# A two-block layer kernel: how the gated attention outputs of blocks one to three are turned from tokens to channels

## The chip, the cores and the metric

The kernel is one program on one core of a Trainium2 chip. The metric is the device time of one launch in microseconds (us). The engines that matter here are TensorE (PE in the rows; its weight load is PEld), VectorE (DVE), ScalarE (ACT), GpSimd (POOL) and SyncE (SP). POOL and SP issue DMA transfers; an engine works its own instructions off in order, and waits between engines go over semaphores.

## The reference, cut to what matters

The reference is a gated delta-rule and convolution block followed by a second block with latent attention. Only the second block's attention branch is touched:

```
h = rmsnorm(x, g);  proj = h @ w_in                      # z_mla is one 2048 wide part of proj
attn = causal_attention(q, k, v)                         # (256 tokens, 16 heads x 128)
attn = attn.reshape(256, 2048) * silu(z_mla)             # the gated attention output
y_mla = attn @ w_o_mla                                   # contracts over the 2048 channels
y_conv = (b_gate * conv * silu(z_conv)) @ w_o_conv
merged = sigmoid(g_mla) * y_mla + sigmoid(g_conv) * y_conv
x = x + rmsnorm(merged @ w_out, g_post)
```

Everything is float32, 256 tokens, model width 2048.

## The kernel before

**Matrix products.** Each product with a 2048 x 2048 weight is cut into 4 column blocks of 512, and each block into 8 *halves*: a half is two row tiles (2 x 128 rows) by 512 columns. A half is 12 matmuls of 128x512: two row tiles, two token tiles of 128, and three products each (hi x hi, hi x lo, lo x hi), since every float32 operand is carried as a high and a low float32r part. The activations stand in `r1h`/`r1l` or `r2h`/`r2l` (128 channels on the partitions, 16 channel tiles, 256 tokens).

**Weights.** SP loads chunks of 1 MB (two halves) into four buffers `raw`; it loads a chunk when DVE is done with the one four before. For each half ACT copies `raw` to `w_hi` (`split` in the scalar block) and DVE writes `w_lo` = `raw` - `w_hi` (`split` in the vector block). In step `hl` of a phase both do the split of half `hl + 3` first (`ahead`, LEAD = 3) and then the other work of that step. ACT may start the split of half h only when PE has finished half h-4 (`w_used`); PE starts half h only when its `w_lo` is there (`lo_ready`).

**The phases around the change**, in PE's order: FC (four rounds; attention heads and the short convolution), FG (gates), FZ (32 halves, the projection z_mla, operand `r2`), YM (32 halves, `w_o_mla`, operand `r1` = the gated attention output), YC (32 halves, `w_o_conv`, operand `r2` = the convolution result, read back from DRAM), OUT (32 halves, operand `r1` = the merged result). "Half 16" below means FZ's half with hl = 16; YM's halves are counted on from FZ's as 32, 33 and so on.

**The work on one block j of z_mla**, before. `at_block(hl, lag)` is j where hl = 8j + 8 + lag. In step 8j+8 ACT makes the tanh of the block's sums from PSUM into `thz` (`half_tanh`, two instructions). In step 8j+9 DVE multiplies (`attn_gate`: two instructions for `gated`, two more with the attention output of the block, which POOL has loaded into `oin[:, j % 2]`), and raises `m_ready`. After half 8j+10 PE waits for `m_ready` and makes 8 transposes of 128x128 (`merged_tr`, through `channels_first`) into two PSUM banks. In step 8j+11 ACT copies them to `r1h` (`merged_hi`) and DVE subtracts into `r1l` (`merged_lo`). For block three (j = 3) these steps fall on halves 32 to 35, that is on the first four of YM. YM's half q (q < 8) waits until `m_lo` shows that channel tiles 2q and 2q+1 are ready.

**The other way of turning.** In YC (and in YA/MIX of the first block) blocks 0 to 2 go another way: POOL writes the 256 x 512 tile to DRAM (`turn_spill`), waits for that write, and reads it back with four transfers (`turn`, `read_quarters`), so that 32-token groups stand on the partitions; one DVE instruction then transposes all 32 x 32 squares (`turned`, 128x1024). The weight columns that make the tile are permuted on the host so that this gives whole channel tiles. ACT's `turned_hi` and DVE's `turned_lo` then make the two parts from SBUF. There ACT and DVE take the tile at lag 7, `turned_lo` at lag 9.

**POOL's order** in FZ: load the four attention blocks into `oin` (the third and the fourth each wait for a block's transposes), load the gain of the last norm, then `reload` the convolution operand into `r2` in four steps, each when PE has gone past half 25, 27, 29 or 31 of FZ.

Of the kernel before, what the change touches and what calls it, by code (L numbers as in the profile page):

```python
# [24 lines left out]
P = 128  # L25
TOK = 256
TT = TOK // P
D = 2048
# [30 lines left out]
TURNS_YC = TURNS_FC + 2 * NJ  # L59
MTR_YA, MTR_ATTN, MTR_Y = 0, 1, 1 + NJ  # L60
# [177 lines left out]
def build_layer(nc, t, out):  # L238
# [38 lines left out]
    with ctx:  # L277
# [145 lines left out]
        with ExitStack() as st:  # L423
            s1 = lambda n, shape, dt=F32: sb(n, shape, dt, st)
            thm, thc = s1("thm", [P, TT, D]), s1("thc", [P, TT, D])
            oin = s1("oin", [P, 2, TT, NB])
            thz = s1("thz", [P, TT, NB])
            assert nc.sbuf_base <= own_end
# [3 lines left out]
        mtmpT = us[:].rearrange("p t h d -> p (t h d)").rearrange("p (a n) -> p a n", a=CT)  # L432
        yT = oin[:, 1].rearrange("p t n -> p (t n)").rearrange("p (a n) -> p a n", a=CT)
# [125 lines left out]
        def _(pool):  # L559
# [267 lines left out]
            pool.wait_ge(sem("m_tr"), MTR_YA + 1)  # L827
# [73 lines left out]
        def _(act):  # L901
# [394 lines left out]
            for hl in range(ph.hn):  # L1296
                ahead(ph, hl)
                if hl == 2:
                    turned_hi(r2h, mtmpT, NJ - 2, OP_M, NJ - 1)
                    merged_hi(r2h, NJ - 1, OP_M, MTR_YA + 1)  # L1300
                if at_block(hl, 0) is not None:
                    mix_block(at_block(hl, 0))
# [199 lines left out]
            for hl in range(ph.hn):  # L1502
                ahead(ph, hl)
                if at_block(hl, 7) is not None and hl < ph.hn - 1:
                    turned_hi(r1h, yT, at_block(hl, 7), OP_Y, NJ - 1 + at_block(hl, 7) + 1)
# [8 lines left out]
            for hl in range(ph.hn):  # L1514
                ahead(ph, hl)
                if hl == 2:
                    turned_hi(r1h, yT, NJ - 2, OP_Y, 2 * (NJ - 1))
                    merged_hi(r1h, NJ - 1, OP_Y, MTR_Y + 1)
                if at_block(hl, 0) is not None:
                    out_block(at_block(hl, 0))  # L1520
# [11 lines left out]
        def _(dve):  # L1532
# [742 lines left out]
            for i in range(ph.iters):  # L2275
                for hl in range(ph.hn):
# [34 lines left out]
                    if hl == 24:  # L2311
                        dve.wait_ge(sem("pv_done"), i + 1)
                        dve.wait_ge(sem("ost_free"), i + 1)
                        sig(V.tensor_tensor(th(ost), banks(0), over(rec[:].rearrange("p t h -> p (t h)"), VD), ALU.mult), "ost_ready", i + 1)
# [70 lines left out]
            for hl in range(PH["YC"].hn):  # L2385
# [5 lines left out]
                if at_block(hl, 7) is not None and hl < PH["YC"].hn - 1:  # L2391
                    merged_turned(yT, oin[:, 0].rearrange("p t n -> p (t n)"), TURNS_YC, at_block(hl, 7), NJ - 1)
# [14 lines left out]
            for hl in range(ph.hn):  # L2407
# [5 lines left out]
                if hl == 1:  # L2413
                    merged_turned(yT, oin[:, 0].rearrange("p t n -> p (t n)"), TURNS_YC, NJ - 2, NJ - 1)
# [30 lines left out]
        def _(pe):  # L2445
# [505 lines left out]
            def heads_tr(hl):  # L2951
                j = at_block(hl, 2)
                if j is not None:
# [66 lines left out]
```

## Time and profile before

| | |
|---|---|
| three runs | 2430.29, 2431.39, 2432.84 us; median 2431.39 |
| the profiled execution's own time | 2431.26 us |
| its span | 2429.7 us |
| mean granted TensorE clock | 0.997 |
| PE busy | 2386.9 us (98%) |
| PEld, DVE, ACT, POOL busy | 1965.0, 1627.4, 1130.7, 225.9 us |
| DMA | 503.68 MB, mean 207 GB/s |

The span is what the trace covers, 1.6 us less than the execution's time. A PE that is busy 98% of the span is followed in almost every half by the next half without a gap, so what an edit is worth shows in two ways only: instructions that leave PE or come to it, and gaps that open or close on PE.

### The profile page before, as it was taken

How to read it: one execution, taken by the hardware profiler on the slowest of the kernel's cores; microseconds unless marked ns; L12 is line 12 of the kernel's file. 1: busy time of each engine (PE TensorE's matmuls, PEld its weight loads, DVE VectorE, ACT ScalarE, POOL GpSimd, SP SyncE). 2: the span in 40 equal slices, each digit the busy share in tenths (PEclk: the TensorE clock that was granted, in tenths of full speed). 3: DMA queues.
4: the chain of work that ended last, by engine and by line, in shares of the span. 5: the costliest groups of instructions: out<-in, count | busy, mean ns of one | idle time of the engine just before them, and what ended most of it. 6: DMA issues, size and time to landing. Idle time of an engine off the chain costs nothing.

```text
span 2429.7 us, 34099 instructions
## 1 busy us (share of the span) xinstructions
PE 2386.9 (98%) x13315; PEld 1965.0 (81%) x13315; DVE 1627.4 (67%) x2173; ACT 1130.7 (47%) x1457; POOL 225.9 (9%) x391
## 2 busy tenths in 40 slices
PE   7999999999999999999999999999999999999998
PEld 6878878787878787878888788888888888888886
DVE  5799999878676776655656665757666544554564
ACT  5444444465453545343455564444444444443443
POOL 3000001112110203011000000010101000000100
PEclk9999999999999999999999999999999999999999
DMA  7566667666454546569655566677667756685673
GB/s 231 194 210 199 199 198 235 220 197 216 156 166 152 186 141 214 185 217 317 224 191 190 168 203 216 223 238 234 217 226 236 245 194 191 208 277 191 223 245 121
DMA packets 237420, 503.68 MB, mean 207 GB/s; under 512 B 14777, under 2 KB 15650, under 8 KB 236130
## 3 DMA queue, kind: packets, MB, share of 16 engines
q1 hardware_dynamic: 214082, 418.57, 52.6%
q0 software_dynamic: 23200, 83.17, 10.5%
q8 instruction: 99, 1.62, 0.3%
q14 instruction: 39, 0.32, 0.0%
HBM read 462.88 MB, written 38.81 MB: 206 GB/s over the span
## 4 chain that ended last, share of the span: by engine, by line
PE 58%; DVE 1%; ACT 1%; DMA 1%; issue 0%; POOL 0%; DVEq 0%; POOLq 0%; ACTq 0%
PE acc L2461 52%; PE acc L2481 2%; PE aux L2644 1%; PE aux L2523 1%; PE acc L2496 0%; PE aux L2924 0%; ACT w_hi L911 0%; DMA qT<-turn_spill 0%; DVE w_lo L1546 0%; DMA turn_spill<-kbe 0%; DVE thm L2428 0%; PE aux L2929 0%; PE aux L2509 0%; DVE kbe L1580 0%; DVE kbe L2031 0%
## 5 line engine op out<-in xcount | busy, mean ns | idle before, releaser
L1546 DVE TENSOR_TENSOR w_lo<-raw,w_hi 128x1024 fp32r<-128x1024 f32 x790 | 963.9, 1224 | 726.5 <-ACT w_hi L911 714.4
L911 ACT CAST w_hi<-raw 128x1024 fp32r<-128x1024 f32 x790 | 826.0, 1050 | 1117.9 <-PE acc L2461 1082.1
L2461 PE MATMUL acc<-w_hi,r1h 128*128 128x512 f32 (+1 forms) x1840 | 728.8, 396 | 8.0 <-DVE w_lo L1546 5.4
L2461 PE MATMUL acc<-w_lo,r1h 128*128 128x512 f32 (+1 forms) x1840 | 714.7, 388 | 0.0
L2461 PE MATMUL acc<-w_hi,r1l 128*128 128x512 f32 (+1 forms) x1840 | 714.4, 388 | 0.0
L2461 PE MATMUL acc<-w_hi,r2h 128*128 128x512 f32 x1208 | 472.3, 391 | 0.3 <-DVE r2l L1641 0.3
L2461 PE MATMUL acc<-w_hi,r2l 128*128 128x512 f32 x1208 | 470.2, 389 | 0.0
L2461 PE MATMUL acc<-w_lo,r2h 128*128 128x512 f32 x1208 | 470.1, 389 | 0.0
L2461 PEld LDWEIGHTS acc<-w_hi,r1h 128*128 128x128 f32 x1840 | 346.0, 188 | 88.0 <-DVE w_lo L1546 8.6
L2461 PEld LDWEIGHTS acc<-w_hi,r1l 128*128 128x128 f32 x1840 | 346.0, 188 | 72.6
L2461 PEld LDWEIGHTS acc<-w_lo,r1h 128*128 128x128 f32 x1840 | 346.4, 188 | 66.6
L2461 PEld LDWEIGHTS acc<-w_hi,r2h 128*128 128x128 f32 x1208 | 226.8, 188 | 48.5 <-issue 1.3
L2461 PEld LDWEIGHTS acc<-w_hi,r2l 128*128 128x128 f32 x1208 | 226.7, 188 | 47.5
L2461 PEld LDWEIGHTS acc<-w_lo,r2h 128*128 128x128 f32 x1208 | 226.8, 188 | 46.3
L1710 DVE SCALAR_TENSOR_TENSOR ycur<-upad,pcw,ycur 128x256 f32<-128x256 f32 x464 | 193.9, 478 | 0.2
L1830 DVE SCALAR_TENSOR_TENSOR cy<-cpad,wq,cy 128x256 f32<-128x256 f32 x144 | 60.7, 480 | 1.0
L2481 PE MATMUL acc<-r1h,w_hi 128*128 128x256 f32 x128 | 36.3, 284 | 1.7 <-DVE r1l L1641 1.7
L2481 PE MATMUL acc<-r1h,w_lo 128*128 128x256 f32 x128 | 36.2, 283 | 0.0
L2481 PE MATMUL acc<-r1l,w_hi 128*128 128x256 f32 x128 | 36.2, 283 | 0.0
L573 POOL TENSOR_SCALAR stat<-stat 128x2 f32<-128x2 f32 (+1 forms) x9 | 5.2, 581 | 306.4 <-DVE stat L2165 94.5
L2481 PEld LDWEIGHTS acc<-r1h,w_hi 128*128 128x128 f32 x128 | 24.5, 192 | 2.1 <-DVE r1l L1641 1.9
L662 POOL DMA_DIRECT2D gate_spill<-gtA x4 | 2.2, 545 | 251.1 <-ACT gtA L1000 251.1
(490 smaller groups left out, 1602.2 us busy)
## 6 DMA issues: line engine op xcount, KB each, us to landing
raw<-in_w_in SPq DMA_DIRECT2D x264, 1024.0 KB, 5.1
raw<-in_w_out SPq DMA_DIRECT2D x32, 1024.0 KB, 5.2
raw<-in_w_br_b SPq DMA_DIRECT2D x16, 1024.0 KB, 5.1
raw<-in_w_br_a SPq DMA_DIRECT2D x16, 1024.0 KB, 7.2
raw<-in_w_ple_gate SPq DMA_DIRECT2D x16, 1024.0 KB, 5.0
raw<-in_w_o_mla SPq DMA_DIRECT2D x16, 1024.0 KB, 5.1
raw<-in_w_o_conv SPq DMA_DIRECT2D x16, 1024.0 KB, 5.0
raw<-in_w_q_b SPq DMA_DIRECT2D x8, 1024.0 KB, 5.0
```

The costliest lines, as they stand in the source:

```text
L573: c.link(g.tensor_scalar(dst, src, scale, EPS, ALU.mult, ALU.add))
L662: pool.dma_start(gate_dram[kind, bass.ds(i, 1)].rearrange("a p n -> p (a n)"), tile[:].rearrange("p t n -> p (t n)")).then_inc(sem("gate_o ...
L911: nc.scalar.copy(w_hi[:, h % HL, 0:n], raw[:, k % RAW, x * HALF:x * HALF + n]).then_inc(hi_ready, 1)
L1546: V.tensor_tensor(w_lo[:, h % HL, 0:n], raw[:, k % RAW, x * HALF:x * HALF + n], w_hi[:, h % HL, 0:n].bitcast(F32), ALU.subtract).then_inc( ...
L1710: c.inc(V.scalar_tensor_tensor(out if k == TAPS - 1 else cur, win, w[:, k:k + 1], cur, ALU.mult, ALU.add))
L1830: c.inc(V.scalar_tensor_tensor(cy[:, h], win, w, cy[:, h], ALU.mult, ALU.add))
L2461: ins = T.matmul(acc[:, s, x, 0:n], a[:, kt0 + k, xs_], w[:, h % HL, at], start=start and k == 0 and m == 0, stop=stop and k == kts - 1 an ...
L2481: ins = T.matmul(acc[:, s, a // 2, a % 2 * TOK:(a % 2 + 1) * TOK], w[:, h % HL, at], o[:, kt0 + k, :], start=start and k == 0 and m == 0 a ...
L2523: ins = T.transpose(X[:, bank + a // 2, (a % 2) * TOK + x * P:(a % 2) * TOK + (x + 1) * P], src(x, a), ident[:])
L2644: ins = T.matmul(X[r, bank, m * SEQ_CHUNK:(m + 1) * SEQ_CHUNK], lhsT(x, h, r), rhs(x, h, r), start=True, stop=True)
```

## The change

The attention outputs of blocks 0 to 2 now go through `turn` as well, and only block 3 keeps PE's transposes. In the order of the program:

- The host permutes the first three 512-column blocks of z_mla's weights, and in FC DVE writes the normalised attention output of rounds 0 to 2 in that permuted order, with two instructions of 128x512 (one for each token tile) in place of one of 128x1024.
- POOL loads attention blocks 0 and 1, then for j = 0, 1, 2: waits for `m_ready` of block j, writes the gated tile to DRAM, waits for the write, reads it back into a new tile `h_land`; and for j = 1, 2 waits for `m_lo` of block j-1 and loads attention block j+1. Only then, and after the transposes of block 3, it loads the gain and issues the convolution operand's reads, all eight without a further wait (PE is past FZ by then).
- DVE in step 8j+16: `merged_turned` (waits for the read back, one transpose instruction of 128x1024 into the old place of the tile in `oin`), before the next block's `attn_gate` in step 8j+17; `turned_lo` behind that gate in the same step.
- ACT in step 8j+16: `turned_hi` (waits for DVE's transpose), then the next block's tanh.
- PE loses the 3 x 8 transposes of blocks 0 to 2, and the waits before them.

The renumbering of semaphore values (MTR_*, TURNED_*, TURNS_*) only follows from this. The core of the diff:

```diff
+            load_attn(0)
+            load_attn(1)
+            for j in range(NJ - 1):
+                pool.wait_ge(sem("m_ready"), OP_ATTN + j + 1)
+                turn(oin[:, j % 2], h_land[:], TURNS_FZ + j + 1)
+                if j:
+                    pool.wait_ge(sem("m_lo"), 2 * (OP_ATTN + j - 1) + 2)
+                    load_attn(j + 1)
+            pool.wait_ge(sem("m_tr"), MTR_ATTN)
             pool.dma_start(gpost2[:], ...)
             pool.wait_ge(sem("cT_out"), 32 * NJ)
             for q in range(NJ):
                 reload(cT_dram, (r2h, r2l), PH["FZ"], 0, q)
...
 # ACT, heads_steps(hl)
+                if at_block(hl, 8) is not None:
+                    turned_hi(r1h, oinT[at_block(hl, 8) % 2], at_block(hl, 8), OP_ATTN, TURNED_ATTN + at_block(hl, 8) + 1)
                 if at_block(hl, 0) is not None:
                     z_tanh2(at_block(hl, 0))
-                if at_block(hl, 3) is not None:
-                    merged_hi(r1h, at_block(hl, 3), OP_ATTN, MTR_ATTN + at_block(hl, 3) + 1)
+                if at_block(hl, 3) == NJ - 1:
+                    merged_hi(r1h, at_block(hl, 3), OP_ATTN, MTR_ATTN)
...
 # DVE, heads_steps(hl)
+                if at_block(hl, 8) is not None:
+                    merged_turned(oinT[at_block(hl, 8) % 2], h_land[:], TURNS_FZ, at_block(hl, 8), TURNED_ATTN)
                 if at_block(hl, 1) is not None:
                     attn_gate(at_block(hl, 1))
-                if at_block(hl, 3) is not None:
+                if at_block(hl, 9) is not None:
+                    turned_lo(r1h, r1l, oinT[at_block(hl, 9) % 2], at_block(hl, 9), OP_ATTN)
+                if at_block(hl, 3) == NJ - 1:
                     merged_lo(r1h, r1l, at_block(hl, 3), OP_ATTN)
...
 # PE
-                if j is not None:
+                if j == NJ - 1:
                     merged_tr(oin[:, j % 2], j, OP_ATTN)
```

ACT's order in FZ, from the tanh of block 0 to that of block 2; before:

```order
L979 ACTIVATE thz<-acc,stat 128x512 x2
L911 CAST w_hi<-raw 128x1024 x3
L1259 ACTIVATE r1h<-aux 128x512 x2
L911 CAST w_hi<-raw 128x1024 x5
L979 ACTIVATE thz<-acc,stat 128x512 x2
L911 CAST w_hi<-raw 128x1024 x3
L1259 ACTIVATE r1h<-aux 128x512 x2
L911 CAST w_hi<-raw 128x1024 x5
L979 ACTIVATE thz<-acc,stat 128x512 x2
```

and now:

```order
L991 ACTIVATE thz<-acc,stat 128x512 x2
L923 CAST w_hi<-raw 128x1024 x8
L1280 ACTIVATE r1h<-oin 128x512 x2
L991 ACTIVATE thz<-acc,stat 128x512 x2
L923 CAST w_hi<-raw 128x1024 x8
L1280 ACTIVATE r1h<-oin 128x512 x2
L991 ACTIVATE thz<-acc,stat 128x512 x2
```

The copies to `r1h` have moved from the middle of a block's eight splits to the place right ahead of the next block's tanh.

DVE's order from the gate of block 2 to that of block 3 and behind it; before:

```order
L2356 SCALAR_TENSOR_TENSOR oin<-thz,stat,oin 128x512
L2357 SCALAR_TENSOR_TENSOR oin<-thz,stat,oin 128x512
L1546 TENSOR_TENSOR w_lo<-raw,w_hi 128x1024 x2
L2037 SCALAR_TENSOR_TENSOR r1l<-aux,r1h 128x512 x2
L1546 TENSOR_TENSOR w_lo<-raw,w_hi 128x1024 x6
L1580 SCALAR_TENSOR_TENSOR thz<-thz,acc 128x512 x2
L2356 SCALAR_TENSOR_TENSOR oin<-thz,stat,oin 128x512
L2357 SCALAR_TENSOR_TENSOR oin<-thz,stat,oin 128x512
L1546 TENSOR_TENSOR w_lo<-raw,w_hi 128x1024 x2
L2037 SCALAR_TENSOR_TENSOR r1l<-aux,r1h 128x512 x2
```

and now:

```order
L2379 SCALAR_TENSOR_TENSOR oin<-thz,stat,oin 128x512
L2380 SCALAR_TENSOR_TENSOR oin<-thz,stat,oin 128x512
L2058 SCALAR_TENSOR_TENSOR r1l<-oin,r1h 128x512 x2
L1560 TENSOR_TENSOR w_lo<-raw,w_hi 128x1024 x7
L1585 STREAM_TRANSPOSE oin<-h_land 128x8x4x32
L1560 TENSOR_TENSOR w_lo<-raw,w_hi 128x1024
L1594 SCALAR_TENSOR_TENSOR thz<-thz,acc 128x512 x2
L2379 SCALAR_TENSOR_TENSOR oin<-thz,stat,oin 128x512
L2380 SCALAR_TENSOR_TENSOR oin<-thz,stat,oin 128x512
L2058 SCALAR_TENSOR_TENSOR r1l<-oin,r1h 128x512 x2
L1560 TENSOR_TENSOR w_lo<-raw,w_hi 128x1024 x2
L2051 SCALAR_TENSOR_TENSOR r1l<-aux,r1h 128x512 x2
```

The low parts of a block (`r1l<-oin`) now stand right behind the next block's gate, and the transpose one split ahead of it.

## Rows read from the trace of the kernel before

**Rows 1.** The page, part 1: busy time of each engine and its share.

```profile
PE 2386.9 (98%) x13315; PEld 1965.0 (81%) x13315; DVE 1627.4 (67%) x2173; ACT 1130.7 (47%) x1457; POOL 225.9 (9%) x391
```

**Rows 2.** Timeline of PE at block 0's transposes: start us, us, what, count.

```profile
2096.63 1.03 PE L2523 MATMUL aux<-ident,oin 128*128 128x128 f32 x8
2097.42 0.48 PE L2461 MATMUL acc<-w_hi,r2h 128*128 128x512 f32 x1
```

**Rows 3.** Timeline of ACT, blocks 1 and 2; in brackets idle time before, and its releaser.

```profile
2111.41 1.05 ACT L911 CAST w_hi<-raw 128x1024 fp32r<-128x1024 f32 x1 [1.67 <-PE acc L2461]
2112.36 1.26 ACT L979 ACTIVATE thz<-acc,stat 128x512 f32<-128x512 f32 x2
2114.13 1.05 ACT L911 CAST w_hi<-raw 128x1024 fp32r<-128x1024 f32 x1 [0.50 <-PE acc L2461]
...
2134.10 1.05 ACT L911 CAST w_hi<-raw 128x1024 fp32r<-128x1024 f32 x1 [1.67 <-PE acc L2461]
```

**Rows 4.** Timeline of DVE over the same halves 16 to 18.

```profile
2112.49 1.23 DVE L1546 TENSOR_TENSOR w_lo<-raw,w_hi 128x1024 fp32r<-128x1024 f32 x1 [1.49 <-ACT w_hi L911]
2115.21 1.23 DVE L1546 TENSOR_TENSOR w_lo<-raw,w_hi 128x1024 fp32r<-128x1024 f32 x1 [1.50 <-ACT w_hi L911]
2116.35 1.28 DVE L1580 SCALAR_TENSOR_TENSOR thz<-thz,acc 128x512 f32<-128x512 f32 x2
...
2118.34 0.74 DVE L2357 SCALAR_TENSOR_TENSOR oin<-thz,stat,oin 128x512 f32<-128x512 f32 x1
2119.11 1.23 DVE L1546 TENSOR_TENSOR w_lo<-raw,w_hi 128x1024 fp32r<-128x1024 f32 x1
```

**Rows 5.** Timeline at block 3: PE's transposes after half 34.

```profile
2164.68 1.03 PE L2523 MATMUL aux<-ident,oin 128*128 128x128 f32 x8
```

**Rows 6.** Timeline at block 3: DVE's last gate instruction ahead of them.

```profile
2163.69 0.75 DVE L2357 SCALAR_TENSOR_TENSOR oin<-thz,stat,oin 128x512 f32<-128x512 f32 x1
```

**Rows 7.** Timeline of DVE in YC, where the tile already goes over DRAM.

```profile
2286.59 1.23 DVE L1546 TENSOR_TENSOR w_lo<-raw,w_hi 128x1024 fp32r<-128x1024 f32 x1 [1.49 <-ACT w_hi L911]
2287.74 1.24 DVE L1571 STREAM_TRANSPOSE oin<-oin 128x1024 f32<-128x1024 f32 x1
...
2296.34 1.41 DVE L2044 SCALAR_TENSOR_TENSOR r1l<-oin,r1h 128x512 fp32r<-128x512 f32 x2
2297.79 3.64 DVE L1546 TENSOR_TENSOR w_lo<-raw,w_hi 128x1024 fp32r<-128x1024 f32 x3
...
2309.93 1.25 DVE L1571 STREAM_TRANSPOSE oin<-oin 128x1024 f32<-128x1024 f32 x1 [0.35 <-DMA oin<-turn_spill]
```

**Rows 8.** Timeline of ACT in YC at the first of those transposes.

```profile
2289.01 1.30 ACT L1268 ACTIVATE r1h<-oin 128x512 fp32r<-128x512 f32 x2 [2.45 <-DVE oin L1571]
2290.34 2.00 ACT L911 CAST w_hi<-raw 128x1024 fp32r<-128x1024 f32 x2
```

**Rows 9.** Timeline of POOL in YC: writes and reads of the turned tile.

```profile
2271.53 0.74 POOL L639 DMA_DIRECT2D turn_spill<-thz  x1 [113.50 <-DVE thz L2377]
2275.53 2.36 POOL L634 DMA_DIRECT2D oin<-turn_spill  x4 [3.27 <-DMA turn_spill<-thz]
2295.46 0.73 POOL L639 DMA_DIRECT2D turn_spill<-thz  x1 [17.57 <-DVE thz L2377]
```

**Rows 10.** Line 634 in 2270 to 2285 us: issue to landing of the first four reads.

```profile
DMA to landing us min/median/max: 4.4/4.5/4.5
```

**Rows 11.** Timeline of POOL in YA: the slowest of the tiles turned there.

```profile
1139.57 0.53 POOL L796 DMA_DIRECT2D ktok<-gate_spill  x1 [13.16 <-DVE kbe L2031]
```

**Rows 12.** Timeline of DVE in YA: the transpose that waited for that tile, a later split.

```profile
1157.05 1.25 DVE L1571 STREAM_TRANSPOSE us<-qT 128x1024 f32<-128x1024 f32 x1 [3.36 <-DMA qT<-turn_spill]
...
1164.52 1.23 DVE L1546 TENSOR_TENSOR w_lo<-raw,w_hi 128x1024 fp32r<-128x1024 f32 x1
```

**Rows 13.** Timeline of PE in YA: what that split held up.

```profile
1164.71 0.39 PE L2461 MATMUL acc<-w_hi,r1l 128*128 128x512 f32 x1
1165.80 0.50 PE L2461 MATMUL acc<-w_hi,r1h 128*128 128x512 f32 x1 [0.70 <-DVE w_lo L1546]
1166.14 0.39 PE L2461 MATMUL acc<-w_lo,r1h 128*128 128x512 f32 x1
```

**Rows 14.** DMA issues of 1118 to 1130 us: KB each, median us to landing.

```profile
raw<-in_w_br_a SPq DMA_DIRECT2D x3, 1024.0 KB, 9.2
```

**Rows 15.** Attention normalisation in FC: duration ns min/median/max of one.

```profile
L2314 DVE TENSOR_TENSOR ost<-aux,rec x4: 1225/1225/1225, 1505.9 to 1849.3; 128x1024 f32<-128x1024 f32 x4
```

More of the change, by code:

```diff
@@ L58 @@
 TURNS_FC = TURNS_YA + NJ - 1
-TURNS_YC = TURNS_FC + 2 * NJ
-MTR_YA, MTR_ATTN, MTR_Y = 0, 1, 1 + NJ
+TURNS_FZ = TURNS_FC + 2 * NJ
+TURNS_YC = TURNS_FZ + NJ - 1
+MTR_YA, MTR_ATTN, MTR_Y = 1, 2, 3
+TURNED_YA, TURNED_ATTN, TURNED_Y = 0, NJ - 1, 2 * (NJ - 1)
 PRAW_LANDED = 2 * 16 * (P // TURN)
@@ L427, in build_layer @@
             thz = s1("thz", [P, TT, NB])
+            h_land = s1("h_land", [P, TT * NB])
             assert nc.sbuf_base <= own_end
@@ L432, in build_layer @@
         mtmpT = us[:].rearrange("p t h d -> p (t h d)").rearrange("p (a n) -> p a n", a=CT)
+        oinT = [oin[:, n].rearrange("p t n -> p (t n)").rearrange("p (a n) -> p a n", a=CT) for n in range(2)]
         yT = oin[:, 1].rearrange("p t n -> p (t n)").rearrange("p (a n) -> p a n", a=CT)
@@ L1504, in _ @@
                 if at_block(hl, 7) is not None and hl < ph.hn - 1:
-                    turned_hi(r1h, yT, at_block(hl, 7), OP_Y, NJ - 1 + at_block(hl, 7) + 1)
+                    turned_hi(r1h, yT, at_block(hl, 7), OP_Y, TURNED_Y + at_block(hl, 7) + 1)
             ph = PH["OUT"]
@@ L1516, in _ @@
                 if hl == 2:
-                    turned_hi(r1h, yT, NJ - 2, OP_Y, 2 * (NJ - 1))
-                    merged_hi(r1h, NJ - 1, OP_Y, MTR_Y + 1)
+                    turned_hi(r1h, yT, NJ - 2, OP_Y, TURNED_Y + NJ - 1)
+                    merged_hi(r1h, NJ - 1, OP_Y, MTR_Y)
                 if at_block(hl, 0) is not None:
@@ L2313, in _ @@
                         dve.wait_ge(sem("ost_free"), i + 1)
-                        sig(V.tensor_tensor(th(ost), banks(0), over(rec[:].rearrange("p t h -> p (t h)"), VD), ALU.mult), "ost_ready", i + 1)
+                        for x in range(TT if i < NJ - 1 else 0):
+                            ins = V.tensor_tensor(ost[:, x].rearrange("p h d -> p (h d)").rearrange("p (q h i) -> p h q i", h=GH, i=TURN),
+                                                  X[:, x].rearrange("p (h q i) -> p h q i", h=GH, i=TURN),
+                                                  rec[:, x].unsqueeze(2).unsqueeze(3).to_broadcast([P, GH, VD // TURN, TURN]), ALU.mult)
+                            if x == 0:
+                                c.inc(ins)
+                        if i == NJ - 1:
+                            ins = V.tensor_tensor(th(ost), banks(0), over(rec[:].rearrange("p t h -> p (t h)"), VD), ALU.mult)
+                        sig(ins, "ost_ready", i + 1)
+                        c.wait()
                     if hl == 24:
@@ L2391, in _ @@
                 if at_block(hl, 7) is not None and hl < PH["YC"].hn - 1:
-                    merged_turned(yT, oin[:, 0].rearrange("p t n -> p (t n)"), TURNS_YC, at_block(hl, 7), NJ - 1)
+                    merged_turned(yT, oin[:, 0].rearrange("p t n -> p (t n)"), TURNS_YC, at_block(hl, 7), TURNED_Y)
                 if at_block(hl, 9) is not None:
@@ L2413, in _ @@
                 if hl == 1:
-                    merged_turned(yT, oin[:, 0].rearrange("p t n -> p (t n)"), TURNS_YC, NJ - 2, NJ - 1)
+                    merged_turned(yT, oin[:, 0].rearrange("p t n -> p (t n)"), TURNS_YC, NJ - 2, TURNED_Y)
                 if hl == 2:
```

10 lines of the change are left out of this document (4 added, 6 removed).

## The prediction

> **What bounds the kernel now.** I read the page's busy times first. PE is busy for 2386.9 of 2429.7 us [rows 1], so a half follows a half with no gap, and an edit counts only by what it takes off PE or by a gap it opens there. Next I read the timelines of PE, ACT and DVE over FZ and the first halves of YM (2088 to 2178 us), where the change sits. The reader should look at the spacing. ACT starts one `w_hi` each 2.72 us (2111.41 to 2114.13, each released by PE [rows 3]); that is the length of a half. Over the eight halves of a block it should be 21.77 us, and it is 22.69 us (2111.41 to 2134.10 [rows 3]). The 0.92 us on top are the 8 transposes: PE starts them at 2096.63 and the next product at 2097.42 [rows 2], 0.79 us later, and the rest goes as the matmuls get back into their stride. There is no wait on PE in this stretch.
>
> I give times as distances from the start of half 16, at 2111.15 us (the `w_hi` that its start releases begins at 2111.41, 0.26 us later). The table that matters, before: `w_hi` of half 19 at 0.26, its `w_lo` at 1.34 (2112.49); tanh of block 1 at 1.21; `w_hi` of half 20 at 2.98; its `w_lo` at 4.06 (2115.21); gate of block 1 from 5.20 (2116.35) to about 7.93 (2118.34 + 0.74) [rows 3, 4]. The `w_lo` of half 19 ends at 2.57 and PE wants it at 8.16: 5.6 us of cover. All that is added to ACT or DVE is hidden up to that cover, and costs PE beyond it.
>
> **Part 1, what PE loses.** 3 blocks x 0.92 us = 2.76 us, on the path, all of it gained. Both ways I can read it (0.79 us at least, 0.92 us with the recovery) come to 2.4 to 2.8 us. PE's waits in front of them cost nothing before, so none goes.
>
> **Part 2, block 0's tile in step 16 (and block 1's in step 24).** DVE's transpose follows `w_lo` of half 19 after 1.15 us, as in YC (2286.59 to 2287.74 [rows 7]): at 2.49. ACT waits for it and starts its two copies 1.27 us later (2287.74 to 2289.01), and is free 1.33 us after that (2290.34) [rows 7, 8]: 3.76 and 5.09. Only now comes the tanh of block 1, which stood at 1.21 before: 3.9 us late. It takes 1.17 us until the next instruction (1.26 us less a small overlap). So `w_hi` of half 20 starts at 6.26 instead of 2.98, its `w_lo` at 7.34, ready at 8.6; PE wants it at 10.88, still in time. The gate of block 1 goes from 8.48 to 11.24 (2.76 us, 2116.35 to 2119.11 [rows 4]), 3.28 us late. Behind it now stands `turned_lo`, 1.45 us (2296.34 to 2297.79 [rows 7]), so `w_lo` of half 21 starts at 12.69. PE can go on 1.28 us after such a start (1164.52 to 1165.80 [rows 12, 13]), at 13.97; half 21 is due at 13.61. That is a gap of 0.36 us, and such a gap costs 0.1 to 0.2 us more until the matmuls are in stride (0.34 us from the first to the second one, in place of 0.23 [rows 13]): **0.5 us**. ACT and DVE have caught up a half later. The same for block 1's tile at half 29: together **1.0 us**. Bounds: if an instruction or two overlap better, 0; if each handover takes 0.1 us more, 2.
>
> **Part 3, block 2's tile in step 32, with block 3 behind it.** Here the same 3.28 us meet a short cover. Block 3 keeps its transposes after half 34. Before, DVE ended its gate at 2164.44 (2163.69 + 0.75 [rows 6]) and PE started the transposes at 2164.68 [rows 5]: 0.24 us of cover. Now the tanh of block 3 stands behind `turned_hi` of block 2 on ACT, and the gate ends 3.28 us later. PE waits 3.28 - 0.24 = 3.04, about **3.1 us** with the handover. While PE stands still DVE catches up: `turned_lo` of block 2 is done 12.7 us after the start of half 32, and half 36, which needs the first part of it, then starts at 14.9. So no second gap. Bounds: 0 if ACT takes the tanh early enough after all (I see no reason in its order), 4 if the delay is a little longer.
>
> **Part 4, the turn itself must be in time.** From `m_ready` POOL needs 0.3 us to start the write; the first reads of YC are issued from 2275.53 on, the last of the four some 1.8 us in, and land 4.5 us after their issue [rows 9, 10]: `m_ready` (2271.2) to landed (2281.8) is 10.6 us. The second took 14.8 us (`m_ready` at 2295.16, 0.3 us before the issue at 2295.46, landed at 2309.93, where DVE had waited 0.35 us [rows 7, 9]). Block 0's `m_ready` is there by 2096.63 [rows 2] and its transpose is due at 2113.64: 17.0 us. For blocks 1 and 2 `m_ready` is 3.28 us late, at 11.2, and the next transpose is due at 22.3 + 2.49 = 24.8: 13.6 us. That is between the two rows. I take "in time", since the mean of the two is 12.7; a wait of y us for block 1 or 2 moves tanh, gate and `w_lo` by y and costs PE y.
>
> [...]
>
> **Part 5, moved reads of the convolution operand.** Eight reads of 512 KB and the gain of 1 MB, 5 MB, now go out in one burst after the transposes of block 3; before they came two at a time. They are wanted in YC, over 80 us later, so only the weights beside them can suffer. A weight chunk is issued when DVE ends a `w_lo` of half h and is wanted by ACT seven halves later, about 16.7 us, and PE has 5.6 us more. Beside a burst of 2.25 MB in YA a chunk landed in 9.2 us (median of three [rows 14]). Cost 0; bounds 0 and, if the chunk takes 25 us, 3. POOL's loads of attention blocks 2 and 3 are issued some 19 us after half 16 or 24 starts and have 11 us; nothing.
>
> **Part 6, FC.** Two instructions of 128x512 from PSUM in place of one of 1.225 us [rows 15]; a 128x512 one with a PSUM operand takes 0.64 to 0.70 us (1.28 for two [rows 4]), so some 0.1 to 0.2 us more on DVE in each of three rounds, under the 5.6 us of cover: 0. If the permuted write were three times as slow, 2.5 us more, it would still be under it.
>
> **Sum.** -2.76 + 1.0 + 3.1 = +1.3 us, against the profiled execution's 2431.26 us: 2432.6; against the median of 2431.39: **2432.7 us**. Measurement can tell about 0.2%, 4.9 us, from no change, so this is no change.
>
> **Rivals.**
> A, the gain stays: the late gate of block 3 is hidden and the gaps of 0.5 us do not open. 2431.4 - 2.8 = 2428.6. For it: DVE and ACT are idle for 1.5 us per half [rows 3, 4]. Against it: 0.24 us of cover at block 3 [rows 5, 6].
> B, the read back is late and ACT, which now waits for it in front of the tanh, hands this on. It decides from 13.6 us. With 14.8 us for both tiles it is 1.2 us each: 2435.1. With the 17.8 us of YA (`m_ready` about 1139.3, 0.3 us before a load [rows 11] that stood ahead of the write; DVE started at 1157.05 after 3.36 us of waiting [rows 12]; there one later half was 0.7 us late [rows 13]) it is about 4 us each: 2432.7 + 8 = **2440.7, slower**. Against the worst: the load that stood ahead of YA's write stands behind the reads here.
> [...]
> C, the burst of part 5 starves the weights: +3, 2435.7.
> D, the transposes are not on the path and their going changes nothing, nor do the waits: 2431.4. The 22.69 us speak against it.
>
> **How the numbers follow.** Forecast (2431 to 2434.5) 0.50; A 0.18; B 0.25, of it half above 2436.3; C 0.05; D 0.02. Faster by over 0.2% (below 2426.5) would need more than the whole of part 1: 0.03, for effects I do not see. Slower by over 0.2% (above 2436.3): 0.12 of B and 0.03 of C: 0.15. Same: 0.82. Range: A with the spread of the runs (about 1.2 us) below, B with one tile badly late above: 2428 to 2437.5.
>
> **What would show it.** Part 1: the spacing of nine `w_hi` starts in FZ's blocks without a gap is 21.8 instead of 22.7 us. Part 2: PE waits for `w_lo` at halves 21 and 29, 0.3 to 0.4 us each; ACT starts the tanh of block 1 some 5.1 us after half 16 starts. Part 3: PE waits about 3 us for DVE's gate ahead of its only transposes of `oin`. Part 4: no DVE wait for `h_land` over 0.5 us. Part 5: weight chunks at YM's start land in under 16 us. Wrong it would be if ACT did the tanh first, if a DVE wait of several us for `h_land` stood there, or if YM lost time to its weights.

## The result: 4.0 us, inside the range, but not by the sum

The changed kernel takes 2434.62 us (median of 22 runs, 2433.47 to 2436.28), the kernel before, timed beside it, 2430.65 us (22 runs, 2429.44 to 2432.84). The ratio is 1.0014, 95% interval 1.0009 to 1.002: 4.0 us more, within 0.2% of no change as forecast, and inside the range. The sum had said 1.3 us, though, and the interval (2.2 to 4.9 us) leaves that out. So a term was mis-sized.

The page of the kernel after, part 1: busy time of each engine (against [rows 1]).

```profile
PE 2388.0 (98%) x13291; PEld 1965.8 (81%) x13291; DVE 1630.4 (67%) x2179; ACT 1131.1 (46%) x1457; POOL 233.5 (10%) x406
```

PE has 24 instructions fewer, the three times 8 transposes, and is 1.1 us *busier*. The same matmuls took longer, which no waiting can do. (A part of this is no effect of the change: this trace also has slow matmuls at the start of FC, at a granted clock of 0.50 from 1443 to 1446 us, which the trace of before has not, at 1.00 there. In the second pair of traces, experiment 10, both kernels have them, and PE is then busy 2387.7 us before and 2387.2 after. In experiment 1, with the same 24 instructions gone and no slow matmuls at either place, it is 2383.5.) The waits show what else is new. In the kernel before, PE has no wait at all from 2060 to 2200 us. In the one after it has this one from 2160 on; columns: who waits, for whom, us in total, times, longest.

```profile
PE aux L2550 <- DVE oin L2380: 3.0, 1, 3.0
```

The same view of after from 2100 to 2130 and from 2130 to 2160 has one line each, and it is the same line: halves 21 and 29.

```profile
PE acc L2488 <- DVE w_lo L1560: 0.3, 1, 0.3
```

How DVE and ACT came to be late stands in their timelines at block 0's tile (start us, us, what, how often, the idle time before it and who ended it). ACT, which in [rows 3] made the tanh first, now waits for DVE's transpose, copies, and only then makes the tanh:

```profile
2110.99 1.05 ACT L923 CAST w_hi<-raw 128x1024 fp32r<-128x1024 f32 x1 [1.67 <-PE acc L2488]
2114.49 1.30 ACT L1280 ACTIVATE r1h<-oin 128x512 fp32r<-128x512 f32 x2 [2.45 <-DVE oin L1585]
2115.82 1.27 ACT L991 ACTIVATE thz<-acc,stat 128x512 f32<-128x512 f32 x2
```

DVE waits for ACT's late `w_hi`, then has the gate, `turned_lo` and four `w_lo` in a row to do (against [rows 4]):

```profile
2113.22 1.24 DVE L1585 STREAM_TRANSPOSE oin<-h_land 128x1024 f32<-128x1024 f32 x1
2118.12 1.23 DVE L1560 TENSOR_TENSOR w_lo<-raw,w_hi 128x1024 fp32r<-128x1024 f32 x1 [3.67 <-ACT w_hi L923]
...
2121.25 0.74 DVE L2380 SCALAR_TENSOR_TENSOR oin<-thz,stat,oin 128x512 f32<-128x512 f32 x1
2122.02 1.42 DVE L2058 SCALAR_TENSOR_TENSOR r1l<-oin,r1h 128x512 fp32r<-128x512 f32 x2
2123.47 4.63 DVE L1560 TENSOR_TENSOR w_lo<-raw,w_hi 128x1024 fp32r<-128x1024 f32 x4
```

The tanh now starts 5.1 us after half 16 does (2115.82 against 2110.73, which is 0.26 us ahead of the `w_hi` that its start releases). All of this is as forecast. What was not forecast stands in PE's timeline at block 3's transposes (against [rows 5]):

```profile
2166.79 1.97 PE L2550 MATMUL aux<-ident,oin 128*128 128x128 f32 x8 [3.03 <-DVE oin L2380]
2168.41 0.78 PE L2488 MATMUL acc<-w_hi,r1h 128*128 128x512 f32 x1
2168.99 0.63 PE L2488 MATMUL acc<-w_lo,r1h 128*128 128x512 f32 x1
2169.41 0.63 PE L2488 MATMUL acc<-w_hi,r1l 128*128 128x512 f32 x1
2169.84 0.50 PE L2488 MATMUL acc<-w_hi,r1h 128*128 128x512 f32 x1
2170.18 0.39 PE L2488 MATMUL acc<-w_lo,r1h 128*128 128x512 f32 x1
```

The stand is 3.03 us, against 3.04 forecast. But the 8 transposes then take 1.62 us to the next product (2166.79 to 2168.41) and not 0.79, and the next products start 0.42 to 0.58 us apart and not 0.23. The windows of after (length, busy us of PE, PEld, DVE, ACT, POOL with counts, PEclk, DMA share, GB/s) say why: the granted clock, in the column before the last two.

```profile
2160.00:2165.00 5.00, 3.76 (x17) 2.79 (x15) 2.13 (x3) 4.73 (x6) 0.00 (x0) 1.00 0.85 327
2165.00:2170.00 5.00, 3.21 (x12) 2.92 (x13) 4.86 (x7) 1.17 (x2) 0.94 (x2) 0.67 0.01 2
2170.00:2175.00 5.00, 5.00 (x24) 4.10 (x23) 3.10 (x4) 1.07 (x2) 3.86 (x8) 0.99 0.96 338
```

TensorE came out of the stand at half speed. In windows of 1 us the granted clock reads 1.00 up to 2166, 0.83 in the next and 0.50 from 2167 to 2170 (0.67 is the mean of a window with all of these). Full speed was back by 2170.18, where the spacing is 0.23 us again (0.97 in the window from 2170, 1.00 in the next).

**The account in us.** Both traces have the same 790 `w_lo` instructions in the same order, one for each half. The difference of their start times, after less before, shows where time is lost or won. From FZ's start on: block 0's missing transposes -0.93; gap at half 21 and block 1's -0.34 (so the gap is 0.59); gap at 29 and block 2's -0.32 (gap 0.60); block 3's place +4.80; then nothing to the end. In all +3.21. Ahead of FZ the traces differ by +0.5: a step of +1.5 at the start of FC, which experiment 10 shows to be no effect of the change, and -1.0 of small differences.

### The profile page after: what moved, and what is told of

Read it like the earlier page. It is cut to its first block, busy times and chain, and to the rows that moved or that the text cites. A ratio compares the mean times of both kernels' runs of the same rounds, so it can differ in the third digit from the quotient of the medians.

```text
span 2433.5 us, 34082 instructions
## 1 busy us (share of the span) xinstructions
PE 2388.0 (98%) x13291; PEld 1965.8 (81%) x13291; DVE 1630.4 (67%) x2179; ACT 1131.1 (46%) x1457; POOL 233.5 (10%) x406
## 3 DMA queue, kind: packets, MB, share of 16 engines
q8 instruction: 99, 1.62, 0.3%
## 4 chain that ended last, share of the span: by engine, by line
PE 58%; DVE 1%; ACT 1%; issue 1%; POOL 0%; DVEq 0%; ACTq 0%; POOLq 0%
PE acc L2488 52%; PE acc L2508 2%; PE aux L2671 1%; PE aux L2550 0%; PE acc L2523 0%; PE aux L2951 0%; DVE w_lo L1560 0%; ACT w_hi L923 0%; DVE thm L2455 0%; PE aux L2956 0%; PE aux L2536 0%; DVE thz L1594 0%; PE aux L2964 0%; PE aux L2965 0%; PE aux L2963 0%
```

## The experiments

Each line "ratio" is against the kernel before on the same chip, with its 95% interval. "The FZ part" is the difference of those `w_lo` starts over FZ and YM, profile against profile of before. Its sign is plus where the kernel is slower than the one before. All are edits of the changed kernel, but for experiments 6 and 9 and the second run of before. Experiment 6 edits the kernel before, experiment 9 that of experiment 1.

**1. The copy one half later.** Only ACT's `turned_hi` moves, so that the tanh no longer stands behind a wait for DVE.

```
-                if at_block(hl, 8) is not None:
-                    turned_hi(r1h, oinT[at_block(hl, 8) % 2], at_block(hl, 8), OP_ATTN, TURNED_ATTN + at_block(hl, 8) + 1)
+                if at_block(hl, 9) is not None:
+                    turned_hi(r1h, oinT[at_block(hl, 9) % 2], at_block(hl, 9), OP_ATTN, TURNED_ATTN + at_block(hl, 9) + 1)
```

> The changed kernel, with one thing moved: ScalarE's copies to r1h of a turned tile stand one step later (step 8j+17 in place of 8j+16), so behind the next block's tanh and the split of one more half. Theory: the whole loss against the kernel before comes from those copies standing ahead of the tanh. Then the gate of block 3 is in time again, PE has no wait ahead of its transposes of block 3 and no wait for w_lo at halves 21 and 29, and all that is left is the 3 x 0.92 us of transposes gained: 2.8 us under the kernel before, some 2427.9 us. Rival (the loss comes from the transfers of the turned tiles, the burst of reads of the convolution operand or the permuted write in FC): those are all still here, so it would stay at 2433 to 2435 us.

Measured: 2428.84 us against 2431.8, ratio 0.9989 (0.998 to 0.9998). The FZ part is -2.77 and PE has no wait between 2060 and 2200. ACT in the changed order:

```profile
2110.17 1.26 ACT L991 ACTIVATE thz<-acc,stat 128x512 f32<-128x512 f32 x2
2111.93 1.05 ACT L923 CAST w_hi<-raw 128x1024 fp32r<-128x1024 f32 x1 [0.51 <-PE acc L2488]
2112.89 1.29 ACT L1280 ACTIVATE r1h<-oin 128x512 fp32r<-128x512 f32 x2
```

The copy now starts with no wait behind a `w_hi`, and block 3's transposes are in time (PE's timeline, with the next product 0.79 us on):

```profile
2160.64 1.04 PE L2550 MATMUL aux<-ident,oin 128*128 128x128 f32 x8
2161.43 0.48 PE L2488 MATMUL acc<-w_hi,r1h 128*128 128x512 f32 x1
```

So all 6.0 us between -2.77 and +3.21 hang on one wait of ACT. Part 1 of the prediction (2.76) is exact, and the kernel is the faster of the two by the interval.

**2. Tanh ahead of the copy, in the same step.** The two ACT statements of step 8j+16 change places.

```
-                if at_block(hl, 8) is not None:
-                    turned_hi(r1h, oinT[at_block(hl, 8) % 2], at_block(hl, 8), OP_ATTN, TURNED_ATTN + at_block(hl, 8) + 1)
                 if at_block(hl, 0) is not None:
                     z_tanh2(at_block(hl, 0))
+                if at_block(hl, 8) is not None:
+                    turned_hi(r1h, oinT[at_block(hl, 8) % 2], at_block(hl, 8), OP_ATTN, TURNED_ATTN + at_block(hl, 8) + 1)
```

> The changed kernel, with ScalarE's tanh of the next block ahead of the copies to r1h, in the same step. The split of half 20 still stands behind the copies, and VectorE's gate behind the w_lo of that split, so the gate is late by 2.1 us, no longer by 3.3. Theory: no wait at halves 21 and 29 (w_lo of half 21 starts at 11.5 us after the start of half 16, wanted by 12.3), and a wait of 1.9 us ahead of block 3's transposes. If the granted clock falls after 1.9 us of idle as it did after 3.0, the time is about that of the kernel before plus 0 to 1 us (2430.6 to 2431.6); if it does not fall, 0.9 us under it (2429.8). Rival (the tanh itself is what counts): no wait at block 3, 2.8 us under the kernel before.

Measured: 2430.03 us, ratio 0.9996 (0.9987 to 1.0005), FZ part -0.70. The gaps at halves 21 and 29 are gone; a shorter stand is left at block 3's transposes:

```profile
2164.82 1.09 PE L2550 MATMUL aux<-ident,oin 128*128 128x128 f32 x8 [1.83 <-DVE oin L2380]
2165.66 0.48 PE L2488 MATMUL acc<-w_hi,r1h 128*128 128x512 f32 x1
```

After 1.83 us the transposes run at full speed in this trace (0.84 us, window clock 1.00), and the place costs 2.07 us (-0.70 + 2.77): the stand and little else.

**3. PE kept busy in the stand.** 13 matmuls on loaded data, whose sums nobody reads, stand where PE waited. This is extra work, added only to hold the clock.

```
+                    for n in range(13):
+                        T.matmul(X[:, 2], r2h[:, 0, 0:P], r2h[:, 0:2].rearrange("p a b -> p (a b)"), start=True, stop=True)
```

> The changed kernel, with 13 products of 128x512 added on TensorE after half 34, ahead of its wait for the gate of block 3; their result goes to an unused PSUM bank and is never read (13 x 0.227 = 2.95 us, as long as the wait was). Theory of the clock: the idle time itself costs 3.0 us, and the 1.7 us that are lost on top of it (the eight transposes take 1.62 us in place of 0.79, the four products behind them 0.4 to 0.6 us each) come from a granted clock that fell while TensorE stood idle; with TensorE busy it does not fall, the transposes take 0.8 us again and the kernel is 1.7 us faster than the changed one: 2432.9 us. Rival (the transposes are slow because their operand has just been written, or because VectorE and ScalarE read PSUM then): they stay slow, 2434.6 us.

Measured: 2433.2 us, ratio 1.0006 (0.9997 to 1.0016), FZ part +1.59 against +3.21 of after. PE's timeline:

```profile
2160.89 3.11 PE L2982 MATMUL aux<-r2h 128*128 128x512 f32 x13
2164.05 1.09 PE L2550 MATMUL aux<-ident,oin 128*128 128x128 f32 x8
2164.89 0.48 PE L2488 MATMUL acc<-w_hi,r1h 128*128 128x512 f32 x1
```

The transposes start 3.16 us after the filler has begun, as late as ever, but take 0.84 us to the next product, and the granted clock stays at full speed, 1.00:

```profile
2160.00:2165.00 5.00, 4.95 (x27) 3.95 (x26) 4.78 (x7) 2.02 (x3) 0.00 (x0) 1.00 0.26 101
```

This is the run that isolates the cause: same lateness, no idle, and 1.6 us come back. The clock's share of the place is thus 1.6 us, the lateness's 3.2. The time of the launches agrees in sign, but its interval alone would not show it, and one trace could be luck, since a clock can also hold through such a stand (experiment 5). The mean granted clock of the launches, on record to three digits for each, speaks against luck. It averages 0.9970 over the 11 launches of this kernel, against 0.9960 over the 22 of after and 0.9961 over the 11 of experiment 7, which has the stand too. The kernels of experiments 1 and 4, which have no such stand, average 0.9965 and 0.9967.

**4. Transposes of block 3 one half later.** PE does half 35 first.

```
-                j = at_block(hl, 2)
+                j = at_block(hl, 3)
```

> The changed kernel, with TensorE's transposes of block 3 after half 35 in place of half 34. The gate ends 11.2 us after half 32 starts, half 35 ends at 10.9: a wait of 0.3 to 0.5 us, too short for the clock to fall. Theory: -2.8 (transposes) + 1.2 (halves 21 and 29) + 0.4 = 1.2 us under the kernel before, 2429.5 us. Rival (the loss is not in that wait): 2433 to 2435 us as the changed kernel.

Measured: 2429.96 us, ratio 0.9994 (0.9985 to 1.0003). The stand shrinks to 0.27 us. The FZ part is -0.29 and not -1.2, and the missing 0.9 us lie elsewhere: in this execution block 1's tile came back late (DVE's timeline) and PE waited 1.1 us for the `w_lo` behind it.

```profile
2134.00 1.25 DVE L1585 STREAM_TRANSPOSE oin<-h_land 128x1024 f32<-128x1024 f32 x1 [0.72 <-DMA h_land<-turn_spill]
```

From `m_ready` at 2119.6 to landed at 2134.0 are 14.4 us, between the two rows of part 4 and over the 13.6 us at hand. That is rival B at its small end. Of the ten profiles with tiles turned in FZ and nothing added to the turn, two show DVE waiting for a tile, this one and that of experiment 7 (0.80 us), both for block 1's; the others none.

**5. Only blocks 0 and 1 turned.** Block 2 goes back to PE's transposes, so the late gate now meets those after half 26.

```
-TURNS_YC = TURNS_FZ + NJ - 1
+TURNS_YC = TURNS_FZ + NJ - 2
...
-                if at_block(hl, 8) is not None:
+                if at_block(hl, 8) in (0, 1):
```

> Only blocks 0 and 1 go over DRAM; blocks 2 and 3 keep TensorE's transposes (weights and the attention output are permuted for two blocks, and the rest follows). Theory: what is late is the gate of whichever block's tanh stands behind a turned block's copies, so the wait of 3.0 us and the half-speed clock move from block 3's transposes (after half 34) to block 2's (after half 26), and half 29 has no gap of its own. -2 x 0.92 + 0.6 + 4.8 = 3.5 us over the kernel before, 2434.2 us. Rival (the wait belongs to YM's start, by the burst or by half 34's place): it stays at block 3's transposes, or is gone with one block less turned there, about 2430 us.

Measured: 2433.66 us, ratio 1.0012 (1.0003 to 1.0021), FZ part +1.91. The stand moved as theory says, to block 2's place, and its length is the same, but its price is not (PE's timeline):

```profile
2143.27 1.10 PE L2552 MATMUL aux<-ident,oin 128*128 128x128 f32 x8 [2.99 <-DVE oin L2382]
2144.12 0.47 PE L2490 MATMUL acc<-w_hi,r2h 128*128 128x512 f32 x1
```

0.85 us to the next product, and a granted clock of 1.00 in every 1 us window from 2139 to 2152: full speed after 2.99 us. The place costs 3.2 us and not 4.8. The launches (2433.66) are near the forecast of 2434.2, the account is not: I had by then taken the clock's fall as what a 3 us stand brings. To see whether this was one lucky execution, the same kernel was run once more:

> The kernel with only blocks one and two turned through DRAM, once more, for one profile. In its first profile TensorE stood 2.99 us ahead of block two's transposes and the eight of them and the next product ran at full speed (next product 0.85 us after the first transpose), while in two profiles of the changed kernel a stand of 3.0 us at block three's was followed by half speed (1.62 us). If the clock is set by the stand's length alone, full speed is seen again here (0.85 us, place cost 3.2 us, span near 2431). If at this length it is chance from one execution to the next, or depends on where the stand falls, this profile may show either; half speed here (1.6 us to the next product, place cost 4.8 us, span near 2432.7) would show that the same program has both.

Measured, one launch: 2432.22 us against 2429.83; FZ part +1.97.

```profile
2142.87 1.09 PE L2552 MATMUL aux<-ident,oin 128*128 128x128 f32 x8 [2.99 <-DVE oin L2382]
2143.72 0.49 PE L2490 MATMUL acc<-w_hi,r2h 128*128 128x512 f32 x1
```

Full speed again (0.85 us, and 1.00 in the same windows), twice out of twice. The 11 launches point the same way: their mean granted clock averages 0.9966, like that of the kernels without a stand. So the length of a stand alone does not tell whether the clock falls.

**6. The reads late, alone.** The kernel *before* with only the late burst of part 5: attention loads as before, the convolution operand's reads behind block 3's transposes, no turn in FZ.

> The kernel before, with one wait added: GpSimd issues the gain's load and the eight reads of the convolution operand only when block 3's transposes are done, all in one burst, as the changed kernel does. All else is as before. Theory: the weight chunks beside the burst take some 11 us to land in place of 5, which their four buffers hide; no change, 2430.7 us, and no wait of TensorE in YM. Rival (the burst is a part of the loss): 1 to 3 us slower.

Measured: 2431.14 us against 2431.08, ratio 0.9999 (0.999 to 1.0008), FZ part -0.07, no wait of PE. The burst is free for PE, though a weight chunk beside it takes 9.5 us to land (median of six; 4.9 in before without the burst, 11.0 in after):

```profile
raw<-in_w_o_mla SPq DMA_DIRECT2D x6, 1024.0 KB, 9.5
```

The cover is not wide, though. The slowest chunk took 13.8 us here and in after, and 17.0 in the trace of experiment 4, where ACT waited 7.2 us in all for chunks at YM's start. PE waited for none of them in any of these traces.

**7. `turned_lo` one half later.** It no longer stands behind the late gate in front of the `w_lo` of halves 21 and 29.

```
-                if at_block(hl, 9) is not None:
-                    turned_lo(r1h, r1l, oinT[at_block(hl, 9) % 2], at_block(hl, 9), OP_ATTN)
+                if at_block(hl, 10) is not None:
+                    turned_lo(r1h, r1l, oinT[at_block(hl, 10) % 2], at_block(hl, 10), OP_ATTN)
```

> The changed kernel, with VectorE's turned_lo one step later (8j+18 in place of 8j+17), so behind the w_lo of one more half. Theory: the waits of 0.3 us for w_lo at halves 21 and 29, which cost 0.56 and 0.61 us with the recovery, are gone, and the wait for the gate of block 3 stays: 1.2 us under the changed kernel, 2433.4 us. Rival (turned_lo is wanted by half 36, or the w_lo of those halves is late for ScalarE's sake alone): no change against the changed kernel.

Measured: 2433.36 us, ratio 1.0009 (1.0 to 1.0018), FZ part +2.28, 0.93 less than after; both gaps are gone (no PE wait from 2060 to 2160), though block 1's tile was 0.80 us late here. The stand at block 3's place, 3.21 us, stays, and here too the clock fell, this time just behind the transposes:

```profile
2165.90 1.09 PE L2550 MATMUL aux<-ident,oin 128*128 128x128 f32 x8 [3.21 <-DVE oin L2380]
2166.75 0.52 PE L2488 MATMUL acc<-w_hi,r1h 128*128 128x512 f32 x1
2167.07 0.63 PE L2488 MATMUL acc<-w_lo,r1h 128*128 128x512 f32 x1
```

The products from 2167.07 on stand 0.43 us apart, at a granted clock of 0.50 to 0.52 up to 2170. The place cost 5.0 us. So a clock at full speed through the transposes is no proof that it holds.

**8. A longer turn.** POOL writes each tile to DRAM twice, one write after the other, before it reads back: what rival B would do if it were large.

```
+                pool.dma_start(gate_dram[0, j], oin[:, j % 2].rearrange("p t n -> p (t n)")).then_inc(sem("extra_out"), 16)
+                pool.wait_ge(sem("extra_out"), 16 * (j + 1))
```

> The changed kernel, with one more write of 512 KB to DRAM ahead of each of the three turned tiles, which GpSimd waits for (to a place that is no longer read): each tile comes back about 4 us later. Theory: what is later than the step in which VectorE wants it goes one to one to TensorE. Block 0 has 17 us and hides it; blocks 1 and 2 have 13.6 us and took up to that, so each is 1.5 to 4 us late: 3 to 8 us over the changed kernel, 2437.5 to 2443 us. Rival (the transfers have cover left and the copies' place in ScalarE's order is all that counts): 2434.6 us as the changed kernel.

Measured: 2448.93 us against 2431.08, ratio 1.0077 (1.0062 to 1.0092): 17.9 us over before, so some 14 over after and not 3 to 8. DVE waits for each tile, 4.00, 3.51 and 3.00 us:

```profile
2116.14 1.25 DVE L1587 STREAM_TRANSPOSE oin<-h_land 128x1024 f32<-128x1024 f32 x1 [4.00 <-DMA h_land<-turn_spill]
```

and one late tile makes PE stand twice, 3 us apart, with the clock at half speed after the second (0.50 from 2128 to 2130 us):

```profile
2122.33 0.50 PE L2490 MATMUL acc<-w_hi,r2h 128*128 128x512 f32 x1 [1.71 <-DVE w_lo L1562]
...
2127.69 0.79 PE L2490 MATMUL acc<-w_hi,r2h 128*128 128x512 f32 x1 [2.30 <-DVE w_lo L1562]
2128.28 0.63 PE L2490 MATMUL acc<-w_lo,r2h 128*128 128x512 f32 x1
```

For the first tile PE waits 4.01 us, 3.7 more than in after. By the `w_lo` starts the first two tiles, 4.00 and 3.51 us late, cost 5.5 and 5.0 us more than in after; the third, whose stand at block 3's place had lost the clock in after already, 2.9 for 3.00 us. The mechanism was right and its price too low: lateness at DVE is passed on one to one, and a clock that falls comes on top, about 1.5 us each time. The forecast was also wrong in how late the tiles would be. It gave block 0 enough cover to hide 4 us, and block 0 had next to none (part 4 below). And the added write did not only add its own 2.9 to 4.6 us: the turn's own write behind it landed 6.4 to 6.9 us after its issue, against 3.1 to 5.1 in after.

**9. The clock elsewhere.** The trace of *before* has a long stand of its own. PE's timeline and windows of before, at the start of QA, a phase ahead of FC:

```profile
1372.88 1.11 PE L2858 MATMUL aux<-ident,mix 128*128 128x128 f32 x4 [3.83 <-DVE mix L2169]
1375.49 0.79 PE L2496 MATMUL acc<-w_hi,r2h 128*128 128x512 f32 x1 [1.50 <-DVE r2l L2184]
```

```profile
1370.00:1375.00 5.00, 1.11 (x4) 0.71 (x4) 2.62 (x6) 1.89 (x7) 1.99 (x4) 0.67 0.01 2
1375.00:1380.00 5.00, 4.51 (x16) 3.61 (x17) 3.49 (x9) 2.39 (x7) 0.00 (x0) 0.65 0.02 3
```

The next kernel is that of experiment 1 with filler matmuls (sums unread): 16 and 6 in that stand and the one behind it, and 7 ahead of FC's first products.

```
+            keep_busy(16, r1h)
             pe.wait_ge(sem("tile0_dve"), TILE0_READY)
             first_tr(0).then_inc(sem("tile0_pe"), 1)
+            keep_busy(6, r1h)
...
+                        if i == 0 and hl == 0:
+                            keep_busy(7, r2h)
```

> The variant that was fastest so far (ScalarE's copies one step later, 2.8 us under the kernel before), with products added on TensorE that nothing reads, at the three places where TensorE waits longest in the middle of the kernel: 16 ahead of the 3.83 us wait for VectorE's first residual block (about 1369 to 1373 us), 6 ahead of the 1.50 us wait behind it, 7 ahead of the 1.7 us wait at the start of FC (about 1441 us). The numbers are chosen so that they end when the wait would have ended (0.227 us each). Theory of the clock: the waits stay as long as they are, but the products behind them come 0.23 us apart in place of 0.43, and the transposes run at full speed: 1.2 us gained at the six slow products, some 0.4 us at the transposes, and up to 1.5 us at FC's start in the runs where the clock falls there. So 1.6 to 3 us under that variant: 4.4 to 5.8 us under the kernel before, 2425 to 2427.5 us. Rival (the clock is none of it, or the added products delay the chain): no change against the variant or slower, 2428 us or more.

Measured: 2427.76 us against 2431.08, ratio 0.9987 (0.9978 to 0.9996): 3.3 us, less than the 4.4 forecast and not to be told from experiment 1. At QA the clock did hold, in the same window as above:

```profile
1375.00:1380.00 5.00, 4.90 (x28) 4.07 (x28) 4.77 (x11) 3.72 (x9) 0.00 (x0) 1.00 0.00 0
```

By the `w_lo` starts 1.8 us were gained there against before and against experiment 1 (2.1 against after), and they are kept up to 1435 us. Then 1.6 us are lost again, and the reason is the place of the seven. They run where PE had nothing to wait for (in after, the first product of FC follows the one before it at 0.23 us), and put it off by their own length:

```profile
1429.66 1.75 PE L2891 MATMUL aux<-r2h 128*128 128x512 f32 x7
1431.25 0.28 PE L2508 MATMUL acc<-r1h,w_hi 128*128 128x256 f32 x1
```

The wait that they were meant to fill comes only 12 us later, with no filler in front of it (PE's timeline, this kernel; 1.74 us in after):

```profile
1443.23 0.38 PE L2508 MATMUL acc<-r1h,w_hi 128*128 128x256 f32 x1 [2.33 <-DVE r1l L1655]
```

Behind it the clock fell in this trace too (0.83 from 1440 to 1450 us), at 1.5 us. So the run shows that the clock can be held, and won time kept, at a second place. It does not show what a filler in FC's stand would bring, since none stood in it.

**10. Both kernels once more**, one launch each:

> The kernel before, unchanged, for a second trace: how far two traces of one program differ ahead of FZ, above all behind the 1.7 us wait at FC's start, where the clock fell in the changed kernel's trace and in one variant's (1.5 us lost) and not in four others. Theory: that is chance, so no difference between programs; here either is possible. Expected 2430 to 2432 us.

> The changed kernel, unchanged, for a second trace. Waits of 0.3, 0.3 and 3.0 us in FZ and YM as in the first one, with the slow transposes, since a wait of 3.0 us is long enough each time; at FC's start the clock may fall or not. Expected 2433 to 2436 us.

Measured: 2431.47 and 2434.22 us, spans 2429.9 and 2432.7. The FZ part of this pair is 3.05 us, the waits of after are the same (0.3, 0.3 and 2.99 us), and the clock fell at the same place (0.50 from 2166 to 2169 us):

```profile
2166.16 1.97 PE L2550 MATMUL aux<-ident,oin 128*128 128x128 f32 x8 [2.99 <-DVE oin L2380]
2167.78 0.78 PE L2488 MATMUL acc<-w_hi,r1h 128*128 128x512 f32 x1
```

The step of 1.5 us at FC's start, which set the first pair apart, is in both kernels here. In the windows from 1440 to 1450, first the first profile of before, then this one:

```profile
1440.00:1450.00 10.00, 8.26 (x66) 7.93 (x65) 6.67 (x13) 5.10 (x10) 0.00 (x0) 1.00 0.82 270
```

```profile
1440.00:1450.00 10.00, 8.26 (x55) 7.97 (x54) 5.25 (x11) 3.63 (x7) 0.00 (x0) 0.83 0.69 220
```

The same kernel, the same stand of 1.74 us, once at full clock and once not.

## Why the prediction came out as it did

**What bounds, and part 1** (-2.76): right to 0.01 us. Experiment 1, where no stand is left, shows -2.77. Rival D is out.

**Part 2** (+1.0): right. Two stands of 0.3 us at halves 21 and 29, costing 0.59 and 0.60 us against 0.5 each. Experiment 7 takes `turned_lo` out from between the gate and that `w_lo`, and both go.

**Part 3** (+3.1): this is the term that failed, in size. Lateness (3.28), place and length of the stand (3.04 forecast, 3.03 measured) were right, and there was no second gap. But the sum took the stand at its length. It cost 4.80 us, above the part's upper bound of 4, since what followed ran at half speed: 0.8 us extra over the transposes and as much over the next four products. Filling the stand with matmuls gave 1.6 us back (experiment 3). The words "4 if the delay is a little longer" bounded the delay and not its consequence. The trace of the kernel before would have shown it: its one stand of like length, 3.83 us, is followed by a window at 0.65. I had read the stretch around the change, and no stretch in which PE stands.

With 1.6 us more the sum is 2.9 us, and the FZ parts of the two pairs of traces are 3.21 and 3.05. The 4.0 us of the launches (2.2 to 4.9) agree with both; the 0.8 us between is not resolved.

**Part 4** (in time): right in both profiles of after, where DVE never waits for `h_land`, but by luck as much as by the sum. The last read of block 2's tile is the fourth of these, issued at 2149.76 us, and lands 8.2 us later, at 2157.93; DVE takes the tile at 2157.95:

```profile
2148.01 2.34 POOL L638 DMA_DIRECT2D h_land<-turn_spill  x4 [2.67 <-DMA turn_spill<-oin]
2157.95 1.25 DVE L1585 STREAM_TRANSPOSE oin<-h_land 128x1024 f32<-128x1024 f32 x1
```

For blocks 0 and 1 the margins are 0.17 and 0.57 us. Block 0's turn took 16.1 us, longer than either row that the forecast went by, and its cover was 16.3 us and not 17.0, since the 17.0 left out that half 16 starts 0.9 us earlier once the transposes are gone. With the 14.4 us of experiment 4, rival B belongs to single executions and to its small end. Its price, y for y, is right for the stand and leaves out the clock (experiment 8).

**Part 5** (0): right, shown alone by experiment 6. Chunks land in 11.0 us (median; 13.8 at most in after), under the 16 forecast. Rival C is out.

**Part 6** (0): nothing was tested alone. Nothing in FC tells the kernels apart: its step of 1.5 us comes and goes in both, and behind it, from 1450 to 2060 us, the `w_lo` starts of after and before keep their distance of 0.5 us.

**Rival A** (2428.6) did not happen as an outcome of this kernel, but it is what the change gives with one statement moved by a half: 2428.84 measured.

## What to carry to other kernels

An engine that works in order should not be made to wait for a neighbour in front of work which that neighbour needs from it: here two copies, needed by nobody for many halves, stood ahead of a tanh that fed a gate, and turned a gain of 2.8 us (experiment 1) into a loss of 3 to 4. A stand of TensorE of some microseconds is to be costed with the clock (here 3.03 us cost 4.80 where it fell, and 2.99 us cost 3.2 where it held), and the price is to be read where the kernel already stands: look at PEclk behind its longest waits before the sum is closed. And filler matmuls must stand in the wait itself: 13 in the stand at block 3's place gave 1.6 us back, and seven put where PE did not wait cost 1.6 us, their own length.

## What the runs showed of the hardware

**When the clock falls.** At block 3's place it fell to 0.50 in all three profiles with a stand of 3 us (2.99, 3.03, 3.21), at block 2's in neither of two (2.99 and 2.99, at 1.00). At FC's start the stand was 1.74 us in 13 profiles (2.33 in the 14th, where it fell too), and the clock fell behind it, to 0.50, in seven of them, at a price of 1.5 us each. At 557 us PE waits for a `w_lo` for 1.3 to 2.1 us in all 14 profiles, and the clock fell there in none (1.00 from 555 to 563 us). After 1.83 us (experiment 2) it held in the trace (1.00), though the mean granted clock of the 11 launches, 0.9962 on average, leaves open whether it does each time. After 2.30 and 2.32 us (experiment 8), each 3 us behind another stand of 1.71 and 1.23, it did not hold (0.50 behind both), and after the 3.8 us at QA's start it was at half speed (0.50) in each of the 13 profiles that have that stand. So in these profiles length alone does not decide between 1.7 and 3 us. At one place, with one length, it differs from one execution to the next, and places differ among themselves. What made the 3 us of experiment 5 harmless twice is open: where it falls, or what ran before it, was not taken apart.

**The turn over DRAM** of a 512 KB tile, beside the weight stream, took 11.5 to 14.4 us from `m_ready` for blocks 1 and 2 in ten profiles, and 12.5 to 16.3 us for block 0. It was in time, by a hair in some, in eight of the ten.

**A burst of 5 MB** of reads doubled a 1 MB weight chunk's landing time (4.9 to 9.5 and 11.0 us) and cost PE nothing, since the chunks are asked for 16.5 to 16.7 us ahead (in before SP issues them at 2165.7, 2171.0 and 2176.3, and ACT takes them at 2182.15, 2187.59 and 2193.03); the slowest took 17.0 us (experiment 4).
